# Hybrid stage of a three-block transformer kernel: the 262 columns of dt and pool first and by token tiles, softplus ahead of the convolution, convolved rows turned inside the product of u0

## The chip, the cores and the metric

One NeuronCore of one Trainium2 chip runs the whole program in one launch. The metric is the device time of one execution in microseconds. TensorE is called PE here, VectorE DVE, ScalarE ACT, GpSimd POOL, and the queue that issues the weight loads SP.

## The reference

256 tokens of 1024 features go through ten stages: ffn, even mixer, ffn, per-layer embedding (ple), ffn, latent attention (mla), ffn, ple, hybrid layer's mixer (hybrid), ffn, and a last norm. The change lies at the border of the second ple stage and in the hybrid stage. Cut to that, in fp32:

```
x = x + rms_norm(sigmoid(h @ w_gate) * (p @ w_proj), post_norm)        # ple, h = rms_norm(x)
u = rmsnorm(x, norm_mix) @ w_in                                        # 1024 x 2694
q, k, v, z, xbc, dt_raw, p_in = split(u, (384, 384, 384, 384, 896, 6, 256))
xbc = silu(causal_depthwise_conv(xbc, conv_w, conv_b))                 # 4 taps, 896 channels
xs, b, c = split(xbc, (384, 256, 256))
dt = softplus(dt_raw + dt_bias);  a_cum = cumsum(dt * -exp(a_log))     # in chunks of 128 tokens
y_ssd  = scan of (xs * dt, b, c, a_cum), gated by silu(z), normed
y_pool = (windowed mean of p_in - p_in) @ pool_w
y_attn = softmax attention of 6 heads over q, k, v
x = x + concat(y_attn, y_ssd, y_pool) @ w_out
```

## The kernel before

**Products.** Every large matmul is done three times, with each operand split in a rounded high part and the rest: low weights by high features, high by high, high by low features (L273 to L275 with tokens as the output's rows, L289 to L291 with features as rows; `hth` and `htl` are the two parts of the turned x, [feature, token]). Weights pass a ring of three slots: SP loads slot n into `raw` as soon as slot n-3 has been split, ACT writes the high part (L234), DVE the low part (L245), each engine in its own written order (`act_ahead.through(n)`, `dve_ahead.through(n)`; `before(n)` means through n+2). ACT may write a ring slot only when PE has used its last content. The first two slots of a stage behind ple are spare ones outside the ring. All order is written by hand, engine by engine; semaphores couple the engines.

**The border ple to ffn and ple to hybrid.** A ple stage ends with its gate product in pieces; DVE then finishes x (L1005, L1011, L1018), tile 0 (tokens 0 to 127) first. Where an ffn stage follows, x is turned by half tiles: PE turns four blocks (`turn_tile`, L407), ACT scales them to `hth` (L414), DVE makes `htl` (L426), and the first product begins with tile 0 while tile 1 is still being made. Where hybrid follows, PE runs 44 transposes of the identity (L937) into a bank that nobody reads, waits until all of x is there, turns it in whole (L357), and ACT and DVE make `hth` and `htl` of both tiles (L377, L390).

**The hybrid stage**, slots counted from its first one, n. PE: n and n+1, the first 512 of the 896 columns of xbc, to banks 4 to 7; the row of 1/rms (L515); n+2 and n+3, the other 384, to banks 0 to 2; n+4 and n+5, the 262 columns of dt and pool, 128x262 in banks 4 and 5; n+6 and n+7 (v and z) to banks 0 and 1, with the turn of the pool rows (L2148) halfway; the turn of the convolved rows (L2160); n+8, n+9 (u0); cumulated sums (L2171); n+10, n+11 with score and pool matmuls halfway; then attention and the output product. DVE: `xa` (L2464) takes banks 4 to 7 out, convolution of those four (L2453, L2456), `xb` (L2472) takes banks 0 to 2 out, convolution of the other three, dt (L2480), the windowed sums of the pool rows (L2489 to L2499), softplus (L2507 to L2516), with the splits of the slots between them. PE writes banks 0 and 1 again with n+6, so it waits for `xb` there.

Of the kernel before, what the change touches and what calls it, by code (L numbers as in the profile page):

```python
# [31 lines left out]
def build_block(nc, io, out):  # L32
# [4 lines left out]
    P = 128  # L37
# [39 lines left out]
    with ExitStack() as stack:  # L77
# [3 lines left out]
        def sem(name):  # L81
            return stack.enter_context(nc.semaphore(name))
# [117 lines left out]
        for s, name in enumerate(PLAN):  # L200
            if name == "mla":
                width[base[s] + 2] = 8 * 192
                for j in (3, 6, 7, 8):
                    width[base[s] + j] = 3 * 384
            if name == "hybrid":
                for j in range(2):
                    width[base[s] + 2 + j] = 4 * 384
                    width[base[s] + 4 + j] = 4 * 262
# [630 lines left out]
        def after_ple(s):  # L839
            return s > 0 and PLAN[s - 1:s + 1] == ["ple", "ffn"]  # L840
# [44 lines left out]

        def ple_pe(pe, s, l):
# [31 lines left out]
            for tt in range(TT):  # L918
                for j in (2, 3):
                    take_slot(pe, n + 1 + j)  # L920
                    pieces = [(kk, half) for kk in range(2) for half in range(2)]
                    if j == 3:
                        pieces.sort(key=lambda v: v[1])
                    for i, (kk, half) in enumerate(pieces):
                        if tt == 1 and j == 3 and i == 3 and after_ple(s + 1):
                            turn_tile(pe, s + 1, 0, 0)
                        m = gate_piece(j, kk, half, tt)
                        if j == 3 and (i == 1 or (i == 3 and tt == 0)):
                            m.then_inc(tile_ready, 1)
                    if tt == 1:  # L930
                        m.then_inc(weights_used, 1)
            if after_ple(s + 1):
                turn_tile(pe, s + 1, 0, 1)
            else:
                pe.wait_ge(ple_gate.sem, ple_gate.after("sigmoid01", l))
                for _ in range(44):
                    nc.tensor.transpose(ps[:, 4, 0:P], ident[:, :], ident[:, :])  # L937

        def ple_act(act, s, l):
# [32 lines left out]
            if after_ple(s + 1):  # L972
                tile_act(act, s + 1, 0, 0, FFN_GAIN[fs[s + 1]])
# [21 lines left out]
        def ple_dve(dve, s, l):  # L995
# [1132 lines left out]
        def hybrid_pe(pe, s):  # L2128
            n = base[s]
            for b in range(4):  # L2130
                turn_x(pe, s, b, b)
            columns_product(pe, n, [bank(4 + j, T) for j in range(4)], 512, first_of=s)
            rms_row_pe(pe, 1, 3)
            columns_product(pe, n + 2, [bank(j, T) for j in range(3)], 384)

            pe.wait_ge(HY_DVE.sem, HY_DVE.after("xa"))
            for half in range(2):
                take_slot(pe, n + 4 + half)
                for kk in range(4):
# [15 lines left out]

            pe.wait_ge(HY_ACT.sem, HY_ACT.after("conv"))
            pe.wait_ge(HY_DVE.sem, HY_DVE.after("dt_raw"))
            for tt in range(TT):
                for k in range(3):
                    nc.tensor.transpose(ps[:, 2 + tt, k * P:(k + 1) * P], h_c[:, k, tt * P:(tt + 1) * P], ident[:, :])  # L2160
            for g in range(SG):
                m = nc.tensor.transpose(ps[:, 2 + g, 3 * P:4 * P], h_c[:, 3 + g, 0:P], ident[:, :])
            HY_PE.done(m, "xs_turned")
            rows_product(pe, n + 8, [bank(4), bank(5)])
# [170 lines left out]
        def hybrid_act(act, s):  # L2335
            n = base[s]
            norm_act(act, s, MIX2)
            HY_ACT.done(nc.scalar.activation(h_ea, a_log[:, :], ACT.Exp), "ea")
            rms(act, s)
            act_ahead.before(act, n + 5)  # L2340
            act.wait_ge(weights_used, n + 6)
            for tt in range(TT):
                m = nc.scalar.activation(h_prow[:, tt, :], ps[:, 4 + tt, SH:SH + HC], ACT.Copy, scale=rstd[:, tt:tt + 1])
            HY_ACT.done(m, "p_rows")
            act_ahead.before(act, n + 6)
# [12 lines left out]
            act.wait_ge(HY_DVE.sem, HY_DVE.after("abs"))  # L2358
            HY_ACT.done(nc.scalar.activation(h_e, h_abs, ACT.Exp, scale=-1.0), "exp_dt")
# [78 lines left out]
        def hybrid_dve(dve, s):  # L2438
            n = base[s]
            norm_dve(dve, s, MIX2)  # L2440
            rms_diagonals(dve, s, 1)
            dve_ahead.before(dve, n + 1)
# [33 lines left out]
            dve_ahead.before(dve, n + 5)  # L2476

            dve.wait_ge(HY_ACT.sem, HY_ACT.after("p_rows"))
            for tt in range(TT):
                m = nc.vector.scalar_tensor_tensor(out=h_raw[:, tt * SH:(tt + 1) * SH], in0=bank(4 + tt, SH),  # L2480
                                                   scalar=rstd[:, tt:tt + 1], in1=dt_bias[:, :], op0=ALU.mult, op1=ALU.add)
            HY_DVE.done(m, "dt_raw")
            dve.wait_ge(HY_DVE.sem, HY_DVE.after("dt_raw"))
            HY_DVE.done(nc.vector.scalar_tensor_tensor(out=h_abs, in0=h_raw, scalar=-1.0, in1=h_raw, op0=ALU.mult, op1=ALU.max), "abs")
# [19 lines left out]


            dve.wait_ge(HY_ACT.sem, HY_ACT.after("exp_dt"))
            dve_link(dve, nc.vector.tensor_scalar(h_s, h_e, 2.0, None, ALU.add))  # L2507
            dve_link(dve, nc.vector.reciprocal(h_s, h_s))
            dve_link(dve, nc.vector.tensor_tensor(h_s, h_s, h_e, ALU.mult))
            dve_link(dve, nc.vector.tensor_tensor(h_s2, h_s, h_s, ALU.mult))  # L2510
            dve_link(dve, nc.vector.tensor_scalar(h_q, h_s2, 1 / 17, None, ALU.mult))
            for d in (15, 13, 11, 9, 7, 5, 3):
                dve_link(dve, nc.vector.scalar_tensor_tensor(out=h_q, in0=h_q, scalar=1 / d, in1=h_s2, op0=ALU.add, op1=ALU.mult))
            dve_link(dve, nc.vector.scalar_tensor_tensor(out=h_q, in0=h_q, scalar=1.0, in1=h_s, op0=ALU.add, op1=ALU.mult))
            dve_link(dve, nc.vector.tensor_scalar(h_raw, h_raw, 0.0, None, ALU.max))
            dve_link(dve, nc.vector.scalar_tensor_tensor(out=h_dt, in0=h_q, scalar=2.0, in1=h_raw, op0=ALU.mult, op1=ALU.add))  # L2516
            dve.wait_ge(HY_ACT.sem, HY_ACT.after("ea"))
            v2 = h_dt.rearrange("p (t h) -> p t h", t=TT)
            HY_DVE.done(nc.vector.scalar_tensor_tensor(out=h_da.rearrange("p (t h) -> p t h", t=TT), in0=v2, scalar=-1.0,
                                                       in1=repeated(h_ea, 1, TT), op0=ALU.mult, op1=ALU.mult), "da")  # L2520
# [335 lines left out]
```

## Time and profile before

| | |
|---|---|
| median of 3 runs | 1346.02 us (1345.81 to 1346.23) |
| the profiled execution, its own time | 1344.6 us |
| its span in the trace | 1342.9 us |
| PE busy | 1318.4 us, 98% of the span |
| DVE, ACT, POOL busy | 63%, 49%, 6% of the span |
| granted TensorE clock, mean | 0.998 |
| ple ends, hybrid begins | at 1034 us of the span |
| attention of hybrid begins | at about 1112 us |

The share of an engine is its busy time by the span. In a timeline row, the first number is the start in microseconds from the span's start, the second the time from the start to the end of the merged group; in square brackets stands idle time of the engine ahead of the row and what ended it.

### The profile page before, as it was taken

To read this page: it belongs to the slowest core of one execution; us is meant where nothing else is said; L and a number is where in the kernel's file an instruction comes from. 1 tells how busy PE (TensorE), PEld (TensorE's weight loads), DVE (VectorE), ACT (ScalarE), POOL (GpSimd) and SP (SyncE) were. 2 spreads that over 40 slices of the span, in tenths; PEclk is the share of its full clock that TensorE was granted. 3 is DMA by queue.
4 is the path that set the end of the run, shared out by engine and by line. 5 is a ranking of instruction groups with operands and counts; after the bars stand their busy time and mean duration, and the time that the engine had idled before them with its cause. 6 is when DMAs were issued, how large, how long until landed. Compare 5 with 4: busy or idle time off the path is not lost.

```text
span 1342.9 us, 17578 instructions
## 1 busy us (share of the span) xinstructions
PE 1318.4 (98%) x6530; PEld 1096.3 (82%) x6530; DVE 846.7 (63%) x926; ACT 651.7 (49%) x756; POOL 81.8 (6%) x185
## 2 busy tenths in 40 slices
PE   8999999999999999999999999999999998999997
PEld 7888889878888888788888877888888986888886
DVE  5555569736655557665556876655557887565554
ACT  5444457424444446644444856444446554544443
POOL 2000003101000001100000300000001200000000
PEclk9999999999999999999999999999999999999999
DMA  8776655424766665476663514776654452576661
GB/s 261 247 235 220 219 188 187 158 63 149 243 219 220 226 231 191 140 237 228 220 225 118 192 55 162 243 223 219 222 200 158 146 187 64 180 243 219 219 228 69
DMA packets 189566, 256.92 MB, mean 191 GB/s; under 512 B 9048, under 2 KB 151022, under 8 KB 189518
## 3 DMA queue, kind: packets, MB, share of 16 engines
q1 hardware_dynamic: 156560, 229.17, 52.2%
q10 hardware_dynamic: 32478, 26.30, 6.1%
q0 software_dynamic: 480, 0.80, 0.4%
q8 instruction: 32, 0.52, 0.2%
q14 instruction: 16, 0.13, 0.0%
HBM read 243.38 MB, written 12.85 MB: 191 GB/s over the span
## 4 chain that ended last, share of the span: by engine, by line
PE 94%; DVE 3%; ACT 1%; issue 0%; DMA 0%; ACTq 0%; DVEq 0%; POOLq 0%; POOL 0%
PE ps L273 28%; PE ps L275 27%; PE ps L274 27%; PE ps L357 1%; PE ps L1130 1%; PE ps L289 1%; PE ps L290 1%; PE ps L291 1%; DVE wl L245 1%; PE ps L1646 1%; PE ps L1645 1%; DVE htl L390 1%; ACT wh L234 0%; PE ps L1226 0%; PE ps L937 0%
## 5 line engine op out<-in xcount | busy, mean ns | idle before, releaser
L273 PE MATMUL ps<-wl,hth 128*128 128x512 f32 (+2 forms) x1264 | 493.6, 391 | 4.2 <-DVE htl L390 2.4
L275 PE MATMUL ps<-wh,htl 128*128 128x512 f32 (+2 forms) x1264 | 487.8, 386 | 0.0
L274 PE MATMUL ps<-wh,hth 128*128 128x512 f32 (+2 forms) x1264 | 487.4, 386 | 0.0
L802 DVE TENSOR_TENSOR wl<-raw,wh 128x2048 fp32r<-128x2048 f32 x120 | 275.1, 2292 | 189.8 <-ACT wh L735 184.5
L735 ACT ACTIVATE wh<-raw 128x2048 fp32r<-128x2048 f32 x120 | 229.7, 1914 | 161.4 <-PE ps L275 84.9
L273 PEld LDWEIGHTS ps<-wl,hth 128*128 128x128 f32 x1264 | 237.4, 188 | 54.7 <-issue 5.3
L275 PEld LDWEIGHTS ps<-wh,htl 128*128 128x128 f32 x1264 | 237.4, 188 | 47.7
L274 PEld LDWEIGHTS ps<-wh,hth 128*128 128x128 f32 x1264 | 237.5, 188 | 45.1
L245 DVE TENSOR_TENSOR wl<-raw,wh 128x2048 fp32r<-128x2048 f32 (+3 forms) x94 | 208.1, 2220 | 70.5 <-ACT wh L234 69.9
L234 ACT ACTIVATE wh<-raw 128x2048 fp32r<-128x2048 f32 (+3 forms) x94 | 173.3, 1852 | 62.3 <-PE ps L275 48.1
L273 PE MATMUL ps<-wl,prod_h 128*128 128x512 f32 x400 | 156.1, 390 | 0.0
L275 PE MATMUL ps<-wh,prod_l 128*128 128x512 f32 x400 | 155.7, 389 | 0.0
L274 PE MATMUL ps<-wh,prod_h 128*128 128x512 f32 x400 | 155.6, 389 | 0.0
L708 ACT ACTIVATE silu_g<-ps,rstd 128x256 f32<-128x256 f32 x110 | 46.3, 472 | 154.1 <-PE ps L275 154.0
L777 DVE SCALAR_TENSOR_TENSOR prod<-ps,rstd,silu_g 128x256 f32<-128x256 f32 x110 | 48.2, 479 | 64.5 <-ACT silu_g L708 64.5
L275 PEld LDWEIGHTS ps<-wh,prod_l 128*128 128x128 f32 x400 | 75.1, 188 | 15.6
L274 PEld LDWEIGHTS ps<-wh,prod_h 128*128 128x128 f32 x400 | 75.1, 188 | 15.5
L273 PEld LDWEIGHTS ps<-wl,prod_h 128*128 128x128 f32 x400 | 75.1, 188 | 15.4
L723 ACT ACTIVATE prod_h<-xn 128x512 fp32r<-128x512 f32 x45 | 28.4, 632 | 93.3 <-DMA xn<-bounce 93.3
L475 POOL TENSOR_SCALAR mean_sq<-mean_sq 128x1 f32<-128x1 f32 x20 | 9.9, 495 | 845.5 <-ACT xn L462 838.7
L377 ACT ACTIVATE hth<-ps,cols 128x256 fp32r<-128x256 f32 x77 | 30.3, 478 | 47.1 <-PE ps L357 47.0
L784 DVE STREAM_TRANSPOSE xn<-prod 128x512 f32<-128x512 f32 x45 | 50.6, 1126 | 1.5
(396 smaller groups left out, 1025.4 us busy)
## 6 DMA issues: line engine op xcount, KB each, us to landing
raw<-in_ffn_w_down SPq DMA_DIRECT2D x88, 512.0 KB, 4.1
raw<-in_ffn_w_gate SPq DMA_DIRECT2D x86, 512.0 KB, 4.0
raw<-in_ffn_w_up SPq DMA_DIRECT2D x86, 512.0 KB, 5.0
raw<-in_w_gate_up SPq DMA_DIRECT2D x44, 512.0 KB, 4.7
raw<-in_even_w_in SPq DMA_DIRECT2D x24, 512.0 KB, 4.7
bounce<-xn ACTq DMA_DIRECT2D x45, 256.0 KB, 2.7
xn<-bounce ACTq DMA_DIRECT2D x45, 256.0 KB, 5.0
raw<-in_w_down SPq DMA_DIRECT2D x22, 512.0 KB, 3.8
```

The lines of the kernel that those rows point to most:

```text
L234: nc.scalar.activation(high_of(n)[:, 0:width[n]], raw[:, n % RING, 0:width[n]], ACT.Copy)\
L245: nc.vector.tensor_tensor(low_of(n)[:, 0:width[n]], raw[:, n % RING, 0:width[n]], high_of(n)[:, 0:width[n]].bitcast(f32), ALU.subtract)\
L273: nc.tensor.matmul(o, xh, b, start=first, stop=False)
L274: nc.tensor.matmul(o, xh, a, start=False, stop=False)
L275: return nc.tensor.matmul(o, xl, a, start=False, stop=last)
L377: m = nc.scalar.activation(dst[:, k, :], ps[:, banks[b], o:o + T], ACT.Copy, scale=g)
L708: nc.scalar.activation(silu_g[:, tt, :], ps[:, b + tt, 0:HC], ACT.Silu, scale=rstd[:, tt:tt + 1]).then_inc(silu_ready, 1)
L723: nc.scalar.activation(prod_tiles(prod_h), moved_tiles, ACT.Copy).then_inc(prod_high, 1)
L735: nc.scalar.activation(wh[:, r, :], raw[:, r, :], ACT.Copy).then_inc(high_ready, 1)
L777: m = nc.vector.scalar_tensor_tensor(out=prod[:, tt, :], in0=ps[:, b + tt, HC:2 * HC], scalar=rstd[:, tt:tt + 1], in1=silu_g[:, tt, :], op ...
L784: nc.vector.transpose(prod_blocks.rearrange("p (r g t) -> p g r t", r=4, g=4), prod[:, :, :].rearrange("p t (k n r) -> p (t k) r n", k=2, ...
L802: nc.vector.tensor_tensor(wl[:, r, :], raw[:, r, :], wh[:, r, :].bitcast(f32), ALU.subtract)\
```

## The change

The 262 columns become slots n and n+1 (now in the spare slots); the xbc columns move to n+2 to n+5. The border to hybrid now turns x by half tiles, as the one to ffn does: 34 of the 44 identity transposes go, 10 stay between the two tiles, and the dt and pool product is done for tile 0 in whole and then for tile 1 (`dt_p`). On DVE dt and softplus move ahead of `xa`, on ACT the exponential of softplus moves ahead of the silu. The turn of the convolved rows (`turn_xs`) moves from between n+7 and n+8 to between n+8 and n+9. `xa`, `xb` and the convolution keep their order; the splits between them are those of the slots that now stand there.

```diff
+        def gain_behind(s):
+            return FFN_GAIN[fs[s]] if PLAN[s] == "ffn" else MIX2
@@ ple_pe
-                        if tt == 1 and j == 3 and i == 3 and after_ple(s + 1):
+                        if tt == 1 and j == 3 and i == 3:
                             turn_tile(pe, s + 1, 0, 0)
...
-            if after_ple(s + 1):
-                turn_tile(pe, s + 1, 0, 1)
-            else:
-                pe.wait_ge(ple_gate.sem, ple_gate.after("sigmoid01", l))
-                for _ in range(44):
-                    nc.tensor.transpose(ps[:, 4, 0:P], ident[:, :], ident[:, :])
+            turn_tile(pe, s + 1, 0, 1)
@@ hybrid_load
-            load_columns(sp, n, w, 1536, 512)
-            load_columns(sp, n + 2, w, 2048, 384)
-            load_columns(sp, n + 4, w, 2432, 262)
+            load_columns(sp, n, w, 2432, 262)
+            load_columns(sp, n + 2, w, 1536, 512)
+            load_columns(sp, n + 4, w, 2048, 384)
@@ hybrid_pe
-            for b in range(4):
-                turn_x(pe, s, b, b)
-            columns_product(pe, n, [bank(4 + j, T) for j in range(4)], 512, first_of=s)
+            def dt_p(tt):
+                for u in range(2):
+                    take_slot(pe, n + u)
+                    for kk in range(4):
+                        k = 4 * u + kk
+                        tile_by(pe, s, tt, k)
+                        m = product(bank(2 * tt, 262), hth[:, k, tt * P:(tt + 1) * P], htl[:, k, tt * P:(tt + 1) * P],
+                                    high_of(n + u)[:, kk * 262:(kk + 1) * 262], low_of(n + u)[:, kk * 262:(kk + 1) * 262],
+                                    k == 0, k == KT - 1)
+                    if tt == TT - 1:
+                        m.then_inc(weights_used, 1)
+
+            dt_p(0)
+            for _ in range(10):
+                nc.tensor.transpose(ps[:, 3, 0:P], ident[:, :], ident[:, :])
+            turn_tile(pe, s, 1, 0)
+            turn_tile(pe, s, 1, 1)
+            dt_p(1)
+            columns_product(pe, n + 2, [bank(4 + j, T) for j in range(4)], 512)
             rms_row_pe(pe, 1, 3)
-            columns_product(pe, n + 2, [bank(j, T) for j in range(3)], 384)
-
-            pe.wait_ge(HY_DVE.sem, HY_DVE.after("xa"))
-            for half in range(2):
-                take_slot(pe, n + 4 + half)
-                for kk in range(4):
-                    m = by_rows([bank(4, 262), bank(5, 262)], 4 * half + kk, n + 4 + half, kk, 262, half + kk == 0, half + kk == 4)
-                m.then_inc(weights_used, 1)
+            pe.wait_ge(HY_ACT.sem, HY_ACT.after("p_rows"))
+            pe.wait_ge(HY_DVE.sem, HY_DVE.after("dt_raw"))
+            columns_product(pe, n + 4, [bank(j, T) for j in range(3)], 384)
...
             pe.wait_ge(HY_DVE.sem, HY_DVE.after("xb"))
             rows_product(pe, n + 6, [bank(0), bank(1)], halfway=turn_p)
-            pe.wait_ge(HY_ACT.sem, HY_ACT.after("conv"))
...
-            rows_product(pe, n + 8, [bank(4), bank(5)])
+            rows_product(pe, n + 8, [bank(4), bank(5)], halfway=turn_xs)
@@ hybrid_dve
-            norm_dve(dve, s, MIX2)
+            for u in range(2):
+                tile_dve(dve, s, 1, u, MIX2)
+            dve_ahead.through(dve, n + 2)
             rms_diagonals(dve, s, 1)
-            dve_ahead.before(dve, n + 1)
+            dve_ahead.through(dve, n + 3)
+            dve.wait_ge(HY_ACT.sem, HY_ACT.after("p_rows"))
...
+            dve_ahead.through(dve, n + 4)
+            dve.wait_ge(HY_ACT.sem, HY_ACT.after("exp_dt"))
...
             rms_row(dve, 1, 3)
...
-            dve_ahead.before(dve, n + 2)
+            dve_ahead.through(dve, n + 5)
...
             convolve(range(4))
-            dve_ahead.before(dve, n + 3)
-            dve.wait_ge(weights_used, n + 4)
+            dve_ahead.through(dve, n + 6)
+            dve.wait_ge(weights_used, n + 6)
...
-            dve_ahead.before(dve, n + 4)
+            dve_ahead.through(dve, n + 7)
```

How the instructions stand now. First PE at the end of ple; `ple_act` is ple's semaphore of ACT, `cols_low` and `pair_low` say that DVE has made half a tile, or its first two blocks, of `htl`. Before:

```order
L275 MATMUL ps<-wh,htl 128x512
L937 MATMUL ps<-ident 128x128 [waits ple_act]
L937 MATMUL ps<-ident 128x128 x43
L357 MATMUL ps<-ident,x_rows 128x128 [waits x_ready]
L357 MATMUL ps<-ident,x_rows 128x128 x3
...
L289 MATMUL ps<-hth,spare_l 128x256 [waits cols_low,split_ready]
```

After the change:

```order
L407 MATMUL ps<-ident,x_rows 128x128 [waits x_ready]
L407 MATMUL ps<-ident,x_rows 128x128 x3
L273 MATMUL ps<-wl,hth 128x512
L274 MATMUL ps<-wh,hth 128x512
L275 MATMUL ps<-wh,htl 128x512
L407 MATMUL ps<-ident,x_rows 128x128 [waits x_ready]
L407 MATMUL ps<-ident,x_rows 128x128 x3
L273 MATMUL ps<-spare_l,hth 128x262 [waits pair_low,split_ready]
```

The block of identity transposes is gone from between ple and hybrid, the first turn stands ahead of the last three matmuls of ple, and the first product of hybrid is the 262-wide one.

Second, DVE from `xa` to `xb`; `wl<-raw,wh` is the low split of a slot, `ps,r_row 128x4x256` is `xa`, `128x3x256` is `xb`. Before:

```order
L2464 TENSOR_TENSOR arena<-ps,r_row 128x4x256 [waits weights_used,r_steps]
L245 TENSOR_TENSOR wl<-raw,wh 128x1048 [waits high_ready]
L2453 TENSOR_SCALAR arena<-arena,conv_cols 128x256 [waits hyb_dve,hyb_pool]
L2453 TENSOR_SCALAR arena<-arena,conv_cols 128x256 x3
L2456 SCALAR_TENSOR_TENSOR arena<-arena,conv_cols 128x256 [waits dve_chain] x12
L245 TENSOR_TENSOR wl<-raw,wh 128x1048 [waits high_ready]
L2472 TENSOR_TENSOR arena<-ps,r_row 128x3x256 [waits weights_used]
```

After the change:

```order
L2495 TENSOR_TENSOR arena<-ps,r_row 128x4x256 [waits weights_used,r_steps]
L245 TENSOR_TENSOR wl<-raw,wh 128x1536 [waits high_ready]
L2484 TENSOR_SCALAR arena<-arena,conv_cols 128x256 [waits hyb_dve,hyb_pool]
L2484 TENSOR_SCALAR arena<-arena,conv_cols 128x256 x3
L2487 SCALAR_TENSOR_TENSOR arena<-arena,conv_cols 128x256 [waits dve_chain] x12
L245 TENSOR_TENSOR wl<-raw,wh 128x2048 [waits high_ready]
L2503 TENSOR_TENSOR arena<-ps,r_row 128x3x256 [waits weights_used]
```

The sequence is the same, but the two splits in it are those of wider slots, n+5 and n+6.

Third, PE at the end of the last xbc product, where n+6 begins. Before:

```order
L289 MATMUL ps<-hth,wl 128x256
L290 MATMUL ps<-hth,wh 128x256
L291 MATMUL ps<-htl,wh 128x256
L273 MATMUL ps<-wl,hth 128x262 [waits split_ready,hyb_dve]
L274 MATMUL ps<-wh,hth 128x262
...
L273 MATMUL ps<-wl,hth 128x512 [waits split_ready,hyb_dve]
```

After the change:

```order
L289 MATMUL ps<-hth,wl 128x256
L290 MATMUL ps<-hth,wh 128x256
L291 MATMUL ps<-htl,wh 128x256
L273 MATMUL ps<-wl,hth 128x512 [waits split_ready,hyb_dve]
L274 MATMUL ps<-wh,hth 128x512
```

The 48 matmuls of width 262 stood between the last xbc product and the wait for `xb`; now nothing does.

## Rows read from the trace of the kernel before

**Rows 1.** Windows: us, then busy us of each engine, clock, DMA share, GB/s.

```profile
1053.35:1096.31 42.96, 42.96 (x267) 38.60 (x266) 42.02 (x75) 25.71 (x28) 1.02 (x4) 1.00 0.56 196
```

**Rows 2.** Timeline of PE, ple to hybrid: start, length, engine, line, operands, count.

```profile
1033.99 4.96 PE L937 MATMUL ps<-ident 128*128 128x128 f32 x44
...
1041.32 0.36 PE L289 MATMUL ps<-hth,spare_l 128*128 128x256 f32 x1 [0.62 <-DVE htl L390]
...
1052.71 0.61 PE L515 MATMUL ps<-silu_g,ones 128*128 128x128 f32 x4
...
1061.79 0.29 PE L273 MATMUL ps<-wl,hth 128*128 128x262 f32 x1
...
1067.60 0.39 PE L273 MATMUL ps<-wl,hth 128*128 128x512 f32 x1
```

**Rows 3.** Timeline of PE at the border ple to ffn at 535 us.

```profile
534.79 0.60 PE L407 MATMUL ps<-ident,x_rows 128*128 128x128 f32 x4
...
535.92 0.60 PE L407 MATMUL ps<-ident,x_rows 128*128 128x128 f32 x4
536.84 0.47 PE L273 MATMUL ps<-spare_l,hth 128*128 128x512 f32 x1 [0.32 <-DVE htl L426]
...
540.96 0.47 PE L273 MATMUL ps<-spare_l,hth 128*128 128x512 f32 x1 [1.12 <-DVE htl L426]
...
543.79 1.04 PE L407 MATMUL ps<-ident,x_rows 128*128 128x128 f32 x8
545.85 0.47 PE L273 MATMUL ps<-spare_l,hth 128*128 128x512 f32 x1 [1.02 <-DVE htl L426]
```

**Rows 4.** Timeline of DVE at the same border.

```profile
540.74 1.40 DVE L1018 SCALAR_TENSOR_TENSOR x_rows<-arena,x_rows 128x512 f32<-128x512 f32 x2
...
547.69 2.28 DVE L245 TENSOR_TENSOR wl<-raw,wh 128x2048 fp32r<-128x2048 f32 x1
```

**Rows 5.** Timeline of DVE in hybrid.

```profile
1047.46 3.52 DVE L245 TENSOR_TENSOR wl<-raw,wh 128x1536 fp32r<-128x1536 f32 x2 [1.45 <-ACT wh L234]
...
1056.11 1.14 DVE L2453 TENSOR_SCALAR arena<-arena,conv_cols 128x256 f32<-128x256 f32 x4
...
1061.92 1.24 DVE L245 TENSOR_TENSOR wl<-raw,wh 128x1048 fp32r<-128x1048 f32 x1
1063.08 0.94 DVE L2472 TENSOR_TENSOR arena<-ps,r_row 128x768 f32<-128x768 f32 x1
1064.00 2.29 DVE L245 TENSOR_TENSOR wl<-raw,wh 128x2048 fp32r<-128x2048 f32 x1
...
1072.77 0.35 DVE L2480 SCALAR_TENSOR_TENSOR arena<-ps,rstd,dt_bias 128x6 f32<-128x6 f32 x2
...
1073.24 2.28 DVE L245 TENSOR_TENSOR wl<-raw,wh 128x2048 fp32r<-128x2048 f32 x1
...
1082.42 2.29 DVE L245 TENSOR_TENSOR wl<-raw,wh 128x2048 fp32r<-128x2048 f32 x1
...
1087.86 0.95 DVE L2524 TENSOR_TENSOR arena<-arena 128x768 f32<-128x768 f32 x1
```

**Rows 6.** Timeline of PE: n+6 halfway, start of u0, cumulated sums.

```profile
1073.09 0.60 PE L2148 MATMUL ps<-ident,arena 128*128 128x128 f32 x4
...
1079.81 0.48 PE L273 MATMUL ps<-wl,hth 128*128 128x512 f32 x1
...
1090.80 2.84 PE L2171 MATMUL ps<-arena 128*128 128x128 f32 x24
```

**Rows 7.** Timeline of ACT: a table load, and the exponential of the decay.

```profile
1070.98 1.28 ACT L2348 ACT_TABLE_LOAD   x1
...
1100.09 1.49 ACT L2365 ACTIVATE arena<-arena 128x1536 f32<-128x1536 f32 x1 [6.02 <-DVE arena L2535]
```

**Rows 8.** Near the start: timeline of PE, and a window with its clock.

```profile
10.02 3.33 PE L357 MATMUL ps<-ident,x_rows 128*128 128x128 f32 x16 [0.45 <-ACT conv_cols L2758]
...
10.00:12.00 2.00, 1.98 (x10) 1.98 (x11) 1.01 (x6) 1.03 (x4) 0.00 (x0) 0.50 1.04 318
```

More of the change, by code:

```diff
@@ L206, in build_block @@
                 for j in range(2):
-                    width[base[s] + 2 + j] = 4 * 384
-                    width[base[s] + 4 + j] = 4 * 262
+                    width[base[s] + j] = 4 * 262
+                    width[base[s] + 4 + j] = 4 * 384
         spare = {base[s] + u: u for s in range(1, len(PLAN)) if PLAN[s - 1] == "ple" for u in range(2)}
@@ L971, in ple_act @@
             sigmoid(1, 0)
[L972 to L973 removed]
+            tile_act(act, s + 1, 0, 0, gain_behind(s + 1))
             sigmoid(1, 1)
@@ L976, in ple_act @@
             squares(1, 1)
-            if not after_ple(s + 1):
-                return
-            tile_act(act, s + 1, 0, 1, FFN_GAIN[fs[s + 1]])
+            tile_act(act, s + 1, 0, 1, gain_behind(s + 1))
             act.wait_ge(ple_vector.sem, ple_vector.after("gained11", l))
@@ L2154, in hybrid_pe, with turn_xs @@
             rows_product(pe, n + 6, [bank(0), bank(1)], halfway=turn_p)
-            pe.wait_ge(HY_ACT.sem, HY_ACT.after("conv"))
[L2157 to L2163, printed above, removed]
-            rows_product(pe, n + 8, [bank(4), bank(5)])
+            def turn_xs():
+                pe.wait_ge(HY_ACT.sem, HY_ACT.after("conv"))
+                for tt in range(TT):
+                    for k in range(3):
+                        nc.tensor.transpose(ps[:, 2 + tt, k * P:(k + 1) * P], h_c[:, k, tt * P:(tt + 1) * P], ident[:, :])
+                for g in range(SG):
+                    m = nc.tensor.transpose(ps[:, 2 + g, 3 * P:4 * P], h_c[:, 3 + g, 0:P], ident[:, :])
+                HY_PE.done(m, "xs_turned")
+            rows_product(pe, n + 8, [bank(4), bank(5)], halfway=turn_xs)
             pe.wait_ge(HY_DVE.sem, HY_DVE.after("da"))
@@ L2336, in hybrid_act @@
             n = base[s]
-            norm_act(act, s, MIX2)
+            norm_tiles_act(act, s, MIX2)
             HY_ACT.done(nc.scalar.activation(h_ea, a_log[:, :], ACT.Exp), "ea")
+            act_ahead.through(act, n + 3)
             rms(act, s)
-            act_ahead.before(act, n + 5)
-            act.wait_ge(weights_used, n + 6)
+            act.wait_ge(weights_used, n + 2)
             for tt in range(TT):
-                m = nc.scalar.activation(h_prow[:, tt, :], ps[:, 4 + tt, SH:SH + HC], ACT.Copy, scale=rstd[:, tt:tt + 1])
+                m = nc.scalar.activation(h_prow[:, tt, :], ps[:, 2 * tt, SH:SH + HC], ACT.Copy, scale=rstd[:, tt:tt + 1])
             HY_ACT.done(m, "p_rows")
+            act_ahead.through(act, n + 4)
+            act.wait_ge(HY_DVE.sem, HY_DVE.after("abs"))
+            HY_ACT.done(nc.scalar.activation(h_e, h_abs, ACT.Exp, scale=-1.0), "exp_dt")
             act_ahead.before(act, n + 6)
@@ L2357, in hybrid_act @@
             HY_ACT.done(nc.scalar.activation(h_b, ps[:, 2:4, 3 * P:4 * P], ACT.Copy), "xs_rows")
-            act.wait_ge(HY_DVE.sem, HY_DVE.after("abs"))
-            HY_ACT.done(nc.scalar.activation(h_e, h_abs, ACT.Exp, scale=-1.0), "exp_dt")
             act_ahead.before(act, n + 9)
@@ L2469, in hybrid_dve @@
             convolve(range(4))
-            dve_ahead.before(dve, n + 3)
-            dve.wait_ge(weights_used, n + 4)
+            dve_ahead.through(dve, n + 6)
+            dve.wait_ge(weights_used, n + 6)
             HY_DVE.done(nc.vector.tensor_tensor(h_x[:, 4:7, PADC:PADC + T], ps[:, 0:3, 0:T], repeated(r_row[:, :], 1, 3), ALU.mult), "xb")
-            dve_ahead.before(dve, n + 4)
+            dve_ahead.through(dve, n + 7)
             dve.wait_ge(HY_DVE.sem, HY_DVE.after("xb"))
             HY_DVE.done(convolve(range(4, XT)), "conv")
[L2476 to L2484, printed above, removed]
+            dve_ahead.before(dve, n + 6)
             dve_ahead.before(dve, n + 6)
@@ L2502, in hybrid_dve @@
             dve_ahead.before(dve, n + 7)
[L2506 to L2520, printed above, removed]
             dve.wait_ge(HY_ACT.sem, HY_ACT.after("xs_rows"))
```

34 lines of the change are left out of this document (26 added, 8 removed).

## The prediction, made before the changed kernel was run

> **What bounds the kernel now.** I read the windows first. From `r_row` to the last split ahead of the decay PE is busy for all of 42.96 us, at clock 1.00, and DVE for 42.02 us of them [rows 1]. So two things set the pace there: PE's own work, and close behind it DVE, whose late work PE meets as soon as the order gives it less cover. A change can therefore gain only what PE loses now, and it loses as soon as it makes PE wait.
>
> Next the timeline of PE at the border. The last product of ple ends at 1033.99; then come 44 identity transposes, the turn of x and its two tiles through ACT and DVE, and the first product of hybrid starts at 1041.32 [rows 2]. That is 7.33 us of PE without a useful matmul but for the turn, and the change rewrites this stretch. The border ple to ffn at 535 us already has the half-tile form that hybrid now gets, so its rows give the durations: the same instructions on x of the same size [rows 3, 4]. Last I read DVE between `xa` and the windowed sums [rows 5].
>
> **The border, part by part.** At the ffn border the turn of the first half tile and ple's last three matmuls take 535.92 - 534.79 = 1.13 us. Three matmuls of width 512 are 0.69 us (24 of them from 1067.60 to 1073.09 [rows 2, 6]), so the turn adds 0.44, and the second turn stands at 1033.99 + 0.44 = 1034.4. Everything at the ffn border is thus shifted by 498.5. First product: 536.84, that is 1035.4. The dt and pool product has 48 matmuls in 1067.60 - 1061.79 = 5.81 us [rows 2], 0.121 each. The first twelve (half a tile of features) run to 1036.8. The next twelve need the second half of tile 0, which in ffn was there at 540.96 [rows 3], so 1039.5: PE idles 2.6 us, more than the 1.12 us in ffn, because these matmuls are half as wide. They end at 1040.9. Ten transposes at 4.96/44 = 0.113 us [rows 2] bring 1042.0. x of tile 1 is ready at 540.74 + 1.40 + 498.5 = 1040.7 [rows 4], so the turn waits for nothing; without the ten it would start 1.1 us sooner. From the turn of tile 1 to the next product ffn takes 545.85 - 543.79 = 2.06 us [rows 3]: 1044.1. Twelve matmuls to 1045.5; the other twelve need the last half tile, which DVE finishes where its split starts, 547.69 - 543.79 = 3.90 us after the turn [rows 3, 4]: 1045.9, plus 0.1 for the semaphore. End of the dt product: 1047.5.
>
> Now the xbc product needs slot n+2. DVE splits it only behind the last half tile, from 1045.9, and the split takes 2.2 to 2.3 us [rows 4]: ready at 1048.2. PE waits 0.7 us more. In the kernel before, the same product starts at 1041.32, and with the 5.81 us of dt put ahead of it that is 1047.1. **Border: +1.1 us.** 34 transposes less are 3.8 us of PE, but PE's path there is not its own work. It is the chain x, turn, high, low of tile 1, and the work on tile 0 now stands on DVE and ACT ahead of the last additions to x. Bounds: if the ten transposes and the wait for n+2 hid, -0.7; if DVE is late with n+3 too, one more split, +3.4.
>
> **Softplus earlier.** On DVE 1087.86 - 1082.42 - 2.29 = 3.2 us [rows 5] of softplus, and 0.47 of dt, go from the busy stretch to the time in which PE runs the first xbc product, 1052.71 - 1041.32 = 11.39 us long [rows 2]. From 1048.2: split of n+3 2.3, dt 0.5, split of n+4 1.76 (half of 3.52 [rows 5]), softplus 3.2, and about 1.4 of waits for ACT by my estimate: done near 1057.4. The cover ends at 1048.2 + 11.4 = 1059.6. Cost nothing; if the cover were gone, at most 3.7 us. The table load that now stands ahead of the decay's exponential is 1.28 us in a place where ACT had been idle for 6.02 [rows 7]; it has no wait of its own in ACT's order, so it runs ahead of it. Cost nothing, at worst 1.3.
>
> **The wait for `xb`.** This is the largest term. Count from the end E of the first xbc product (before: 1052.71 [rows 2]). `xa` and one split were done, and the convolution started, at 1056.11, E + 3.40. The split in front of it is now that of n+5, 1536 wide, 1.76 instead of 1.24 us: E + 3.92. The convolution of four tiles takes 1061.92 - 1056.11 = 5.81: E + 9.73. The next split is now n+6, 2048 wide, 2.2: E + 11.95. `xb` 0.94: E + 12.9 [rows 5]. PE has the row of rms and the second xbc product in 1061.79 - 1052.71 = 9.08 us [rows 2], and then wants banks 0 and 1 for n+6. Before, the 5.81 us of dt lay there as cover (9.08 + 5.81 = 14.9, and `xb` ended at 1064.0, E + 11.3). Now there is none. **PE waits 12.9 - 9.1 = 3.8 us**, and its queue is in order: n+6, n+7 and all behind them wait too. The inputs of the splits are no later: ACT may write n+5 and n+6 by E.
>
> **The next one.** From the end of `xb` to the end of the split of n+9 DVE has what it had from 1064.00 to 1082.42, 18.42 us with three splits in it, less the 0.47 of dt: 17.95. PE from n+6 to its need of n+9 has 1079.81 - 1067.60 = 12.2 with both turns, and half of 1090.80 - 1079.81: 17.7 [rows 2, 5, 6]. Wait: 0.3. The turn of the convolved rows inside u0 is the same eight transposes; it gives ACT's silu 5.5 us more time and costs nothing, but `xs_rows` is later, close to when the cumulated sums want nothing of banks 2 and 3: cost 0 to 0.8. From n+9 on DVE waits for ACT's split of n+12, which waits for u0 on PE, as before, so all keeps its distance and is only shifted.
>
> **Sum:** 1.1 + 3.8 + 0.3 = +5.2 us. Against the profiled execution's own 1344.6 that is 1349.8; that execution lies 1.4 under the median of 1346.02, so against the median it is 1351.2.
>
> **Rivals.** (a) The clock falls in the new waits. Two of them, 2.6 and 3.8 us, are longer than any within the border to ffn (1.12 [rows 3]). Near the start, 16 transposes took 3.33 us at a granted clock of 0.50 [rows 8], 0.208 each against 0.113 at full clock: one such stretch costs 16 x 0.095 = 1.5 us, and two of them, with the 0.3 swallowed, 2.7: 1353.9. Against it: behind the gap of 1.12 us at the ffn border the next twelve matmuls take 543.79 - 540.96 = 2.83 us [rows 3], 0.236 each, full clock, and the ten transposes stand in the first one. The Trainium skill, page TensorE: Matmul & The Clock Gate, section HAM oscillation, says that waits between bursts of matmuls send the clock back to half, and each burst starts cold; by it this case would be the rule. (b) More is late than I see (the split of n+3, a weight load, ACT's rows of pool): one more split of 2.3 us, 1353.5. (c) The wait for `xb` is covered after all, because DVE comes to `xa` with its splits already done; only the border is left: 1347.1, and no difference could be told. Against it: the order of DVE is written, and both splits stand behind `xa`. (d) Faster: what PE does itself is all that counts, and with 34 transposes less at 0.113 the time is 1342.2. That PE is busy for all of the 42.96 us [rows 1] speaks for it. It decides if `xb` ends within 9.1 us of E instead of 12.9 and the low half of tile 1 by 1042; the rows give 1045.9.
>
> **Numbers.** The bound under which no difference can be told here is 0.2%, 2.7 us. Forecast 0.54 (its own range 1349.8 to 1352.5), (a) 0.18, (b) 0.10, (c) 0.12, (d) 0.06. Slower: 0.54 + 0.18 + 0.10 = 0.82; same 0.12; faster 0.06. The range goes from just under (c), since part of the wait may be covered, to just over (a): 1346.8 to 1354.4.
>
> **What would show it.** In the timeline of PE after: a gap of about 2.6 us before the thirteenth 262-wide matmul; 0.7 us at the first 128x256 matmul, ended by DVE's split; a gap of 3.8 us at the first 128x512 matmul of n+6, ended by `xb`, and not by the split; a small one at n+9. PE's busy time falls by 3.8 and its idle time grows by 9. If instead PE starts n+6 with no wait, the mechanism is wrong; if PE starts the xbc product before 1047, the border is; if matmuls of 128x512 come at twice the 0.229 us of before behind the gap, (a) it is.

## The result

| | before | changed |
|---|---|---|
| median | 1345.95 us (4 runs, 1345.81 to 1346.23) | 1353.66 us (4 runs, 1353.04 to 1354.13) |
| ratio to before | | 1.0059, 95% interval 1.0045 to 1.0074 |
| profiled execution, own time / span | 1344.6 / 1342.9 us | 1354.13 / 1352.4 us |
| mean granted clock | 0.998 | 0.994 |

The change costs 7.7 us. One of the seven runs of the kernel before in the first set of experiments took 2677.09 us and counts in no ratio.

The spans of the two profiled executions differ by 9.5, of which 1.3 lie ahead of the first product of the program: the profile of before had got its full clock sooner there, and all kernels built from the changed one but one were within 0.7 us of it at the second ple's end. So I measure from a mark in the program, the second half-tile turn behind ple (before: where it would stand, 1033.99 + 0.44 = 1034.43 [rows 2]), to the cumulated sums.

The timeline of PE in the changed kernel, from ple's end to the cumulated sums. L407 is the turn of a half tile, L2137 the ten identity transposes, L515 the row of rms behind the first xbc product, L2152 the turn of the pool rows halfway through n+6, L2176 the cumulated sums:

```profile
1035.75 0.60 PE L407 MATMUL ps<-ident,x_rows 128*128 128x128 f32 x4
1036.67 0.36 PE L273 MATMUL ps<-spare_l,hth 128*128 128x262 f32 x1 [0.32 <-DVE htl L426]
...
1040.79 0.36 PE L273 MATMUL ps<-spare_l,hth 128*128 128x262 f32 x1 [2.43 <-DVE htl L426]
...
1042.33 1.25 PE L2137 MATMUL ps<-ident 128*128 128x128 f32 x10
1043.42 1.04 PE L407 MATMUL ps<-ident,x_rows 128*128 128x128 f32 x8
1045.47 0.36 PE L273 MATMUL ps<-spare_l,hth 128*128 128x262 f32 x1 [1.02 <-DVE htl L426]
...
1047.54 0.36 PE L273 MATMUL ps<-spare_l,hth 128*128 128x262 f32 x1 [0.37 <-DVE htl L426]
...
1049.65 0.39 PE L289 MATMUL ps<-hth,wl 128*128 128x256 f32 x1 [0.41 <-DVE wl L245]
...
1061.26 0.61 PE L515 MATMUL ps<-silu_g,ones 128*128 128x128 f32 x4
...
1074.18 0.79 PE L273 MATMUL ps<-wl,hth 128*128 128x512 f32 x1 [3.68 <-DVE arena L2503]
...
1082.65 0.60 PE L2152 MATMUL ps<-ident,arena 128*128 128x128 f32 x4
...
1100.34 2.84 PE L2176 MATMUL ps<-arena 128*128 128x128 f32 x24
```

The brackets hold the idle time ahead of the row and who ended it. The first bracket over 2 us is the wait for the second half of tile 0, the one of 3.68 us is the wait for `xb` (L2503). Piece by piece against [rows 2, 6]:

| piece | before | changed | difference |
|---|---|---|---|
| mark to the first xbc product, with dt's 5.81 us counted in both | 6.89 + 5.81 = 12.70 | 1049.65 - 1035.75 = 13.90 | +1.20 |
| first xbc product | 11.39 | 1061.26 - 1049.65 = 11.61 | +0.22 |
| its end to n+6, dt not counted | 9.08 | 1074.18 - 1061.26 = 12.92 | +3.84 |
| first half of n+6 | 1073.09 - 1067.60 = 5.49 | 1082.65 - 1074.18 = 8.47 | +2.98 |
| from there to the cumulated sums | 17.71 | 17.69 | -0.02 |
| sum | | | +8.22 |

The fourth piece is the clock, as this execution has it; how much it costs differs from one execution to the next (run 3). The windows of the changed kernel show it; the number before the last two is the granted clock:

```profile
1060.00:1070.00 10.00, 10.00 (x86) 10.00 (x86) 8.06 (x17) 3.83 (x2) 0.97 (x3) 1.00 0.36 118
1070.00:1074.00 4.00, 0.50 (x5) 0.29 (x3) 4.00 (x5) 3.19 (x2) 0.00 (x0) 0.94 0.00 0
1074.00:1076.00 2.00, 1.82 (x4) 1.49 (x5) 2.00 (x2) 0.00 (x0) 0.00 (x0) 0.50 0.79 203
1076.00:1080.00 4.00, 4.00 (x11) 3.08 (x10) 4.00 (x12) 0.00 (x0) 0.00 (x0) 0.50 1.03 356
1080.00:1084.00 4.00, 4.00 (x20) 3.28 (x19) 3.57 (x4) 3.29 (x8) 0.00 (x0) 0.95 0.20 75
```

From 1070 to 1074 PE is busy for 0.50 of 4 us and DVE for all 4. Late in that wait the clock falls (0.78 in 1073 to 1074), and PE then works at 0.50, 1.2 GHz, until just after 1080, where the same stretch before was at 1.00.

Who keeps PE waiting is seen on DVE. Its timeline in the changed kernel, `r_row` (L520) and `xa` (L2495) to `xb` (L2503), to be read beside [rows 5]:

```profile
1061.90 0.42 DVE L520 COPY r_row<-ps 128x256 f32<-128x256 f32 x1 [3.49 <-PE ps L515]
1062.36 1.23 DVE L2495 TENSOR_TENSOR arena<-ps,r_row 128x1024 f32<-128x1024 f32 x1
1063.50 1.75 DVE L245 TENSOR_TENSOR wl<-raw,wh 128x1536 fp32r<-128x1536 f32 x1
1065.17 1.14 DVE L2484 TENSOR_SCALAR arena<-arena,conv_cols 128x256 f32<-128x256 f32 x4
1066.22 4.84 DVE L2487 SCALAR_TENSOR_TENSOR arena<-arena,conv_cols 128x256 f32<-128x256 f32 x12
1070.97 2.29 DVE L245 TENSOR_TENSOR wl<-raw,wh 128x2048 fp32r<-128x2048 f32 x1
1073.17 0.96 DVE L2503 TENSOR_TENSOR arena<-ps,r_row 128x768 f32<-128x768 f32 x1
```

Behind `r_row` no bracket stands in it: DVE works without a pause, and PE starts when `xb` ends. PE itself was through with the second xbc product 3.7 us earlier.

### The profile page after: what moved, and what is told of

Its sections match the earlier page's. It is cut to its first block, busy times and chain, and to the rows that moved or that the text cites. A ratio compares the mean times of both kernels' runs of the same rounds, so it can differ in the third digit from the quotient of the medians.

```text
span 1352.4 us, 17528 instructions
## 1 busy us (share of the span) xinstructions
PE 1319.5 (98%) x6496; PEld 1095.6 (81%) x6496; DVE 848.5 (63%) x934; ACT 652.5 (48%) x764; POOL 82.2 (6%) x185
## 4 chain that ended last, share of the span: by engine, by line
PE 93%; DVE 4%; ACT 2%; issue 1%; DMA 0%; ACTq 0%; DVEq 0%; POOLq 0%; POOL 0%
PE ps L273 28%; PE ps L275 27%; PE ps L274 27%; DVE wl L245 1%; PE ps L357 1%; PE ps L1123 1%; PE ps L289 1%; PE ps L290 1%; PE ps L291 1%; PE ps L1639 1%; PE ps L1638 1%; DVE htl L390 0%; ACT hth L414 0%; DVE htl L426 0%; ACT wh L234 0%
## 5 line engine op out<-in xcount | busy, mean ns | idle before, releaser
L245 DVE TENSOR_TENSOR wl<-raw,wh 128x2048 fp32r<-128x2048 f32 (+2 forms) x94 | 210.3, 2243 | 69.9 <-ACT wh L234 69.1
L234 ACT ACTIVATE wh<-raw 128x2048 fp32r<-128x2048 f32 (+2 forms) x94 | 175.1, 1870 | 60.9 <-PE ps L275 43.8
L790 DVE TENSOR_TENSOR prod_l<-xn,prod_h 128x512 fp32r<-128x512 f32 x45 | 31.1, 691 | 38.6 <-ACT prod_h L723 38.6
```

What stands on the lines that cost most here:

```text
L234: nc.scalar.activation(high_of(n)[:, 0:width[n]], raw[:, n % RING, 0:width[n]], ACT.Copy)\
L245: nc.vector.tensor_tensor(low_of(n)[:, 0:width[n]], raw[:, n % RING, 0:width[n]], high_of(n)[:, 0:width[n]].bitcast(f32), ALU.subtract)\
L790: nc.vector.tensor_tensor(prod_tiles(prod_l), moved_tiles, prod_tiles(prod_h).bitcast(f32), ALU.subtract).then_inc(prod_low, 1)
```

## The experiments

All runs were compared with the kernel before on the same chip; its median was 1345.67 in the first set and 1345.53 in the other two. The theory: the loss is not in PE's own work. The change made PE run into DVE's written order (at `xb`), and the idle time there also brings the clock down; the border is a chain through x of tile 1. The rivals stand with each run.

**1. Keep PE at work in the wait.**

```diff
+            pe.wait_ge(HY_DVE.sem, HY_DVE.after("xa"))
+            for _ in range(30):
+                nc.tensor.transpose(ps[:, 7, 0:P], ident[:, :], ident[:, :])
             pe.wait_ge(HY_DVE.sem, HY_DVE.after("xb"))
```

> The changed kernel with 30 transposes of the identity on PE (3.4 us of work, into a bank nobody reads) inside the wait for xb. Theory: the wait itself stays (first matmul of n+6 still 12.9 us behind the first xbc product), but the clock no longer falls in it, so the first half of n+6 takes 5.5 us instead of the 8.5 seen in the changed kernel: 1353.7 - 3.0 = 1350.7. Rival: the slow matmuls behind the wait have another cause than the idle time (DVE and weight loads in the same stretch), then they stay slow and the time stays 1353.7.

Measured: 1352.36 (1351.74 to 1353.12), ratio to before 1.0052 (1.0034 to 1.0070). The timeline of PE around the wait:

```profile
1061.40 0.61 PE L515 MATMUL ps<-silu_g,ones 128*128 128x128 f32 x4
...
1070.49 3.44 PE L2159 MATMUL ps<-ident 128*128 128x128 f32 x30
...
1074.33 0.50 PE L273 MATMUL ps<-wl,hth 128*128 128x512 f32 x1 [0.41 <-DVE arena L2506]
...
1079.95 0.60 PE L2152 MATMUL ps<-ident,arena 128*128 128x128 f32 x4
```

n+6 still starts 12.93 us behind L515, but its first half takes 5.62 us, not 8.47, and mark to cumulated sums (1035.91 to 1097.86) is 2.64 us shorter. So the slow matmuls came from the idle time, which settles that rival. The median fell by only 1.3 of the expected 3.0. Part of it is the choice of executions: the profiled one of the changed kernel was its slowest of four, the profiled one here the fastest of four, and these two differ by 2.4. Run 3 shows that the clock can also cost less than 3.0 behind the same wait. How the 1.3 comes about in the medians isn't shown.

**2. Take `xb` out of PE's way with other banks**, v and z in banks 4 and 5, u0 in 6 and 7.

```diff
-            pe.wait_ge(HY_DVE.sem, HY_DVE.after("xb"))
-            rows_product(pe, n + 6, [bank(0), bank(1)], halfway=turn_p)
+            pe.wait_ge(HY_DVE.sem, HY_DVE.after("xa"))
+            rows_product(pe, n + 6, [bank(4), bank(5)], halfway=turn_p)
...
-            rows_product(pe, n + 8, [bank(4), bank(5)], halfway=turn_xs)
+            pe.wait_ge(HY_DVE.sem, HY_DVE.after("tail"))
+            rows_product(pe, n + 8, [bank(6), bank(7)], halfway=turn_xs)
```

> The changed kernel with v and z in banks 4 and 5 and u0 in banks 6 and 7, so that PE needs xa but no longer xb at n+6; DVE's order is the same. Theory: only xb itself (0.9 us) leaves the wait, for the split of n+6 stands ahead of it on DVE and ends 12.0 us behind the first xbc product, where PE comes at 9.1: gap 2.8 instead of 3.7, time 1352.8 if the clock still falls, 1349.8 if it does not. Rival: xb is what PE waits for, and without it the whole gap goes: 1347.

Measured: 1352.93 (1351.81 to 1353.08), ratio 1.0052 (1.0034 to 1.0070). The row at n+6, and two windows:

```profile
1074.37 0.47 PE L273 MATMUL ps<-wl,hth 128*128 128x512 f32 x1 [2.91 <-DVE wl L245]
```

```profile
1034.00:1050.00 16.00, 11.88 (x78) 10.91 (x76) 10.16 (x24) 12.03 (x30) 5.01 (x6) 0.89 0.01 2
1074.00:1078.00 4.00, 3.63 (x11) 2.96 (x12) 4.00 (x7) 0.76 (x1) 0.00 (x0) 0.70 0.67 203
```

The gap is 2.91 instead of 3.68 and now ends with the split of n+6, as the theory had it: behind `xb` stood the whole written order. The rival, that the whole gap goes and the time is 1347, is refuted. The clock still fell (0.70 from 1074), but the first half of n+6 took 1081.55 - 1074.37 = 7.18 us and not 8.47. In this execution it had fallen at the border too (0.89). There it fell only after PE had started again behind the gap of 2.43 us at 1040.11 (1.00 in 1040 to 1041, 0.73 in 1041 to 1042, 0.50 in 1042 to 1044), and the ten transposes took 2.34 us instead of 1.25; mark to first xbc product is 15.53 us instead of 13.90.

**3. Without the ten transposes of the border.**

```diff
             dt_p(0)
-            for _ in range(10):
-                nc.tensor.transpose(ps[:, 3, 0:P], ident[:, :], ident[:, :])
             turn_tile(pe, s, 1, 0)
```

> The changed kernel without the ten identity transposes between the tiles. Theory: they lie on PE's path, the turn of tile 1 starts 1.1 us sooner and the split of n+2 too: 1353.7 - 1.1 = 1352.6. Rival: they keep the clock up at the border, and without them it falls there: 1.5 to 3 us slower, 1355 to 1357. Other rival: x of tile 1 is ready no sooner, no change.

Measured: 1352.18 (1352.08 to 1352.25), ratio 1.0049 (1.0031 to 1.0067): 1.5 us under the changed kernel. Mark to first xbc product is 1048.85 - 1036.07 = 12.78 instead of 13.90, so the ten lay on the path with all of their 1.1 us. The window from 1034 to 1050 had clock 1.00; they were not needed for it in this execution, and all four times lie far under the 1355 to 1357 of the rival.

The rows at n+6 show something more, in a place that the edit did not touch:

```profile
1073.39 0.50 PE L273 MATMUL ps<-wl,hth 128*128 128x512 f32 x1 [3.68 <-DVE arena L2501]
...
1080.58 0.60 PE L2150 MATMUL ps<-ident,arena 128*128 128x128 f32 x4
```

The wait is the same 3.68 us as in the changed kernel, but the first half of n+6 takes 7.19 us and not 8.47. The clock fell only after PE had started again (1.00 in 1073 to 1074, 0.55 in 1074 to 1075) and was back at 1.00 from 1078 on. So the same wait cost 1.7 us of clock here and 2.98 in the changed kernel, and with run 2 (1.7) two of three profiled executions show the lower price.

**4. The banks of run 2, and the split of n+6 ahead of the first convolution.**

```diff
+            dve_ahead.through(dve, n + 6)
             convolve(range(4))
-            dve_ahead.through(dve, n + 6)
```

> As the kernel with the other banks, and DVE splits n+6 ahead of the convolution of the first four tiles. Theory that DVE as a whole is what PE runs into: no wait and no clock fall at n+6 (gap gone, 6.6 us gained against the changed kernel), but DVE's 7 us of windowed sums and the second convolution still stand ahead of the splits of n+8 and n+9, so PE waits about 1.3 us at n+8 and 2.5 to 3 at n+9: 1351 to 1352. Rival, that the wait at n+6 is the only trouble: waits of under 0.5 us in all, 1347.2.

Measured: 1351.95 (1351.45 to 1352.13), ratio 1.0046 (1.0028 to 1.0064). No row with a bracket at n+6, and two later:

```profile
1084.02 0.50 PE L273 MATMUL ps<-wl,hth 128*128 128x512 f32 x1 [1.42 <-DVE arena L2513]
...
1092.62 0.50 PE L273 MATMUL ps<-wl,hth 128*128 128x512 f32 x1 [1.99 <-DVE wl L245]
```

The first is n+8, which waits for the copy of the pool rows out of bank 6 (a wait that my choice of banks brought in), the second n+9 and its split, which stands behind the windowed sums. The wait had only moved, 1.42 + 1.99 = 3.4 us of it. The clock stayed at 1.00 in both. The rival of 1347.2 is refuted.

**5. DVE's order mended behind it.** The windowed sums, wanted by nobody before the pool product, go behind the splits of n+8 and n+9, and ACT splits n+9 ahead of its silu.

```diff
             dve_ahead.through(dve, n + 7)
-            dve.wait_ge(HY_DVE.sem, HY_DVE.after("xb"))
-            HY_DVE.done(convolve(range(4, XT)), "conv")
...
             dve.wait_ge(HY_PE.sem, HY_PE.after("p_turned"))
             HY_DVE.done(nc.vector.tensor_copy(h_p[:, :, PADP:PADP + T], bank(6).rearrange("p (k t) -> p k t", k=2)), "tail")
+            dve_ahead.through(dve, n + 8)
             dve.wait_ge(HY_DVE.sem, HY_DVE.after("tail"))
+            HY_DVE.done(convolve(range(4, XT)), "conv")
+            dve_ahead.through(dve, n + 9)
```

> The kernel with the other banks and the early split of n+6, and DVE's order mended behind it: the copy of the pool rows, then the split of n+8, the second convolution and the split of n+9, and only then the windowed sums, which nothing wants before the pool product; ACT splits n+9 ahead of the silu. Theory that all the loss behind the border is DVE standing in PE's way in the written order: no wait of PE over 0.3 us from the first xbc product to the cumulated sums, no clock fall there, and only the border's 1.2 us is left: 1347. Rival, that DVE has too much work in this stretch in any order: the waits come back at n+10, n+11 or the decay, 1349 to 1351.

Measured: 1347.52 (11 runs, 1346.94 to 1350.15), ratio 1.0016 (1.0007 to 1.0025). The windows show DVE as full as in [rows 1] and PE without a gap:

```profile
1062.00:1074.00 12.00, 12.00 (x88) 11.38 (x87) 11.96 (x21) 5.31 (x3) 0.93 (x3) 1.00 0.51 176
1074.00:1090.00 16.00, 16.00 (x77) 13.15 (x76) 15.69 (x25) 9.41 (x15) 0.00 (x0) 1.00 0.57 196
1090.00:1102.00 12.00, 12.00 (x69) 10.48 (x68) 11.83 (x13) 7.62 (x6) 0.00 (x0) 1.00 0.39 133
```

About 6 us of the 7.7 came back by order and banks alone. What is left is 2.0 us in the medians. From the mark to the cumulated sums it is 58.00 against 56.37 us, 1.6 more, and 1.2 of that is the border and 0.2 the first xbc product. The rival, that the waits come back later (1349 to 1351), is refuted.

**6. The same without the ten transposes**, with the edit of run 3.

> The same without the ten identity transposes at the border. By the run that took only these away, 1.0 us less: 1346, level with the kernel before. Rival: the clock falls at the border more often without them, 1347.5 to 1349.

Measured: 1346.83 (11 runs, 1345.96 to 1347.15), ratio 1.0009 (1.0000 to 1.0018); 0.7 less than run 5, where 1.0 was expected. The rival, a clock that falls more often and 1347.5 to 1349, is refuted.

**7. The border in another order:** on DVE at the end of ple the last additions to x go first, and on PE tile 1 is turned between the two halves of tile 0's dt product. ACT's squares go behind its part of tile 1. The three go together, so this run doesn't tell what each of them is worth.

```diff
+            if PLAN[s + 1] == "hybrid":
+                add(1)
+                tile_dve(dve, s + 1, 0, 1, gain_behind(s + 1))
+                return
...
-            dt_p(0)
+            dt_p(0, (0,))
             turn_tile(pe, s, 1, 0)
             turn_tile(pe, s, 1, 1)
+            dt_p(0, (1,))
             dt_p(1)
```

> The same, and at the border DVE finishes x of tile 1 ahead of the low half of tile 0, PE turns tile 1 ahead of the second half of the dt product of tile 0, and ACT splits n+2 and turns tile 1 ahead of the two sums of squares. Theory that the border is the chain x, turn, high, low of tile 1 and the split of n+2: x of tile 1 is there 0.9 to 1.1 us sooner and the first xbc product with it: 1345, 0.7 under the kernel before. Rival: another chain (rms, whose squares are now later, or DVE's split) takes its place: no gain over the run without the ten, 1346.

Measured: 1345.42 (11 runs, 1345.02 to 1346.16), ratio 0.9998 (0.9989 to 1.0007): level with the kernel before, 1.4 under run 6. Mark to the end of the first xbc product is 23.98 us (before: 24.09; changed: 25.51; run 6: 24.42), with the clock at 0.89 in 1034 to 1050:

```profile
1039.55 1.32 PE L407 MATMUL ps<-ident,x_rows 128*128 128x128 f32 x8 [2.08 <-DVE x_rows L1016]
1041.34 0.50 PE L273 MATMUL ps<-spare_l,hth 128*128 128x262 f32 x1 [0.47 <-DVE htl L426]
```

The clock fell behind the turns, not in them: it was 1.00 in 1039 to 1041 and 0.50 in 1042 to 1044, and the first fifteen matmuls of width 262, from 1041.34 to 1044.69, came 0.22 us apart instead of 0.12, which is about 1.5 us. The path in this profile is only 0.4 us shorter than in run 6, the medians 1.4; the difference isn't explained.

**8. The same with 16 identity transposes in the wait for x of tile 1.**

```diff
             dt_p(0, (0,))
+            for _ in range(16):
+                nc.tensor.transpose(ps[:, 4, 0:P], ident[:, :], ident[:, :])
             turn_tile(pe, s, 1, 0)
```

> The kernel with the border in the order tile 1 before the second half of tile 0's dt product, and 16 identity transposes (1.8 us) where PE idles 2.08 us for x of tile 1. Theory: the half clock seen at this border (eight turns in 1.32 us instead of 0.87, granted clock 0.89 in 1034 to 1050) is gone, and the path has 1.1 to 1.5 us less: 1344.2, 1.3 us under the kernel before. Rival: these transposes delay the turn, or the slow stretch was chance and most runs have none: no change, 1345.4.

Measured: 1345.26 (11 runs, 1343.98 to 1345.46), ratio 0.9995 (0.9986 to 1.0004). The window from 1034 to 1050 shows clock 1.00, and the mark to the end of the first xbc product is 1058.76 - 1036.14 = 22.62 us, 1.4 shorter than in run 7.

```profile
1040.83 1.32 PE L407 MATMUL ps<-ident,x_rows 128*128 128x128 f32 x8 [0.33 <-DVE x_rows L1016]
```

The eight turns take 1.32 us here too, at clock 1.00, so the expectation was wrong to count them as slowed by the clock. The times don't show the shorter path: 0.16 us under run 7, on another chip, where 1.3 under the kernel before was expected, and where the rival (most executions of run 7 had no slow stretch) said 1345.4. The medians side with the rival; only one execution of each was profiled, which can't prove it. From the mark to the cumulated sums this execution is 1.3 us shorter than before's, the median 0.3. Whether it beats the kernel before stays open.

**9. Softplus back to its old place**, in the kernel of run 5. The dt rows and `abs` stay early; the 15 small operations move.

```diff
             HY_DVE.done(nc.vector.scalar_tensor_tensor(out=h_abs, in0=h_raw, scalar=-1.0, in1=h_raw, op0=ALU.mult, op1=ALU.max), "abs")
             dve_ahead.through(dve, n + 4)
-            dve.wait_ge(HY_ACT.sem, HY_ACT.after("exp_dt"))
-            dve_link(dve, nc.vector.tensor_scalar(h_s, h_e, 2.0, None, ALU.add))
...
             HY_DVE.done(m, "diff")
             dve_ahead.before(dve, n + 7)
+            dve.wait_ge(HY_ACT.sem, HY_ACT.after("exp_dt"))
+            dve_link(dve, nc.vector.tensor_scalar(h_s, h_e, 2.0, None, ALU.add))
...
```

> The kernel with other banks and mended DVE order (1347.5, with the ten transposes), but softplus back where it stood in the kernel before, behind the windowed sums. Theory: from r_row to the decay DVE is full (98% busy) and its 3.2 us of softplus come out on PE's path, at the cumulated sums, which want da, and at n+10: 1350.6. Rival: PE has slack against da and the splits there, as in the kernel before, where PE waited for neither: 1347.5.

Measured: 1351.39 (5 runs, 1350.23 to 1352.09), ratio 1.0041 (1.0027 to 1.0054), against 1.0016 in run 5. The timeline of PE:

```profile
1095.83 2.94 PE L2177 MATMUL ps<-arena 128*128 128x128 f32 x24 [1.52 <-DVE arena L2523]
...
1099.93 0.47 PE L273 MATMUL ps<-wl,hth 128*128 128x512 f32 x1 [0.81 <-DVE wl L245]
...
1107.91 1.09 PE L2205 MATMUL ps<-ident,arena 128*128 128x128 f32 x8 [0.48 <-DVE arena L2539]
```

PE waits 1.52 for `da`, 0.81 for the split of n+10, 0.48 for the decay, 2.8 in all. Measured from the mark, this execution stands 3.2 us behind that of run 5 when the decay's turns begin (L2205), and the medians are 3.9 apart; the rest isn't placed. The rival, 1347.5, is refuted. So in the order of run 5 the early softplus is worth 3 to 4 us: it takes 3.2 us out of a stretch in which DVE is full, and lays it into one where DVE had been idle. It is no gain against the kernel before, which had softplus late and made PE wait for nothing there [rows 1].

## Why the prediction was right, and what it missed

Forecast 1351.2 with a range of 1346.8 to 1354.4; measured 1353.66. The direction, the places of the waits and their lengths were right. The time lies in the range only because its top was set by rival (a): the forecast's own case reached from 1349.8 to 1352.5 and left the clock out.

- **Border, +1.1:** right, +1.20. The gap of 2.6 us ahead of the thirteenth 262-wide matmul was 2.43; the 0.7 at n+2's split was 0.41, because the dt product ended 0.3 later. That the ten transposes lie on the path is shown by run 3.
- **The wait for `xb`, +3.8:** right, +3.84. `xb` ended as counted, 12.9 us behind the first xbc product. Rival (c), that DVE would come there with its splits done, is refuted by the rows of DVE above.
- **n+9, +0.3:** it was 0. In the changed kernel PE was so late by the clock that DVE was 2.2 us ahead of it. But run 1, where the wait for `xb` stood and the clock held, has no wait there either: the split of n+9 ended at 1092.22, 17.95 us behind `xb` as counted, and PE came at 1092.28, 17.95 us behind its start of n+6 (1074.33), where 17.7 had been counted. So the term was 0.3 too large by itself. The mechanism is real: with the clock and the wait at n+6 gone, run 4 shows 1.99 us there.
- **Softplus and table load at nothing:** right. DVE was through with softplus 3.5 us before `r_row` wanted it, and the table load took 1.28 us at 1103.62, where ACT still waited 4.72 us for the decay behind it. Run 9 gives the price of softplus in the full stretch.
- **Rival (a), the clock,** had a chance of 0.18 and was the case at `xb`. This is the step that failed: "Forecast 0.54" was given to the case without it, on the ground that the border to ffn shows no slowing with gaps of 1.12 us. The wait for `xb` is three times as long and nothing ran in it. The size was off as well: the 16 transposes at half clock of [rows 8] gave 1.5 us, but the half clock lasted from the end of the wait until past 1080, matmuls of width 512 coming 0.43 us apart, and cost 2.98. The 1.7 us of runs 2 and 3 are near the 1.5. That the 1353.9 of this rival lies so close to the time is luck: it counted two falls of 1.5 us, and the profile has one, of 2.98, and none at the border. There the clock fell in one of the first five profiles. The rule of the Trainium skill (TensorE: Matmul & The Clock Gate, HAM oscillation), that bursts behind a wait start cold, was weighed in the prediction and set below the row. At `xb` the changed kernel agrees with it (0.50 from the first matmul on); in runs 2 and 3 the burst started at 1.00 and fell to 0.50 about 1 us later; at the border most executions kept 1.00.
- **The sum:** 1.1 + 3.8 + 0.3 = 5.2 was forecast for 8.2 on the path and 7.7 in the medians. On the path, 3.0 of the missing part is the clock and 0.2 the first xbc product, which from the ring's slots took 0.121 us a matmul and from the spare ones 0.119 (why isn't shown); the 0.3 of n+9 goes off. Only one of the four executions of the changed kernel was profiled, its slowest, so how much of the 7.7 is clock in the others isn't shown.
- **The signs:** of those named, the gaps at the thirteenth matmul, at the xbc product and at n+6 came, ended as foretold; the one at n+9 didn't. PE's idle time from the mark to the cumulated sums grew from 0.6 to 8.2 us, not by 9, and its busy time grew by 0.6 instead of falling by 3.8, in part because the slow matmuls of n+6 count as busy.
- **"The end of `xb` is PE's need":** the wait was named after the instruction that came last, though its sum was made of all that stands ahead of it. Run 2 shows that the whole of DVE's order is behind the name, since without `xb` 2.9 us remain.

## What to carry to other kernels

A product that waits for nothing is cover for the engine behind it. Before you move it, look up which wait stands next in PE's order, and count the releasing engine's written order up to it, splits of later slots included. A wait that a change opens can cost more than its length, since the clock may fall with it (here 1.7 to 3.0 us on top of 2.9 to 3.7). And where an engine is 98% busy beside PE, taking one wait away moves it to the next; work that nobody wants yet (here the windowed sums) is what has to go back.

## What the runs showed of the hardware

A wait of PE of 3.68 us was followed by a granted clock of 0.50 in both profiled executions that had it empty; it cost 2.98 us in the changed kernel, where the clock fell before the wait was over, and 1.7 us in run 3, where it fell after PE had started again. A wait of 2.91 us (run 2) did the same for 1.7 us. The wait filled with 30 identity transposes cost nothing of the kind (5.62 us for the stretch instead of 8.47).

Gaps of 2.1 to 2.4 us at the border were followed by a fall in some profiled executions (0.89 in the window of 16 us in runs 2 and 7, there too only after PE had started again) and by none in the others (1.00 in the changed kernel and in runs 1, 3, 4, 5, 6 and 9; in run 8 the gap was filled). Behind the gaps of 1.42 and 1.99 us in run 4 and of 1.52, 0.81 and 0.48 us in run 9 the clock stayed at 1.00.
